# Two heads per transpose and four tiles per product group in the chunked scan of a two-block model

## The reference, cut to what matters

```python
def wkv_scan(s0, r, decay, k, v, kk, b, reverse, emit):
    def step(s, inp):
        r_t, w_t, k_t, v_t, kk_t, b_t = inp
        sa = jnp.einsum('bhij,bhj->bhi', s, kk_t)
        s = s * w_t[:, :, None, :] - sa[..., None] * b_t[:, :, None, :] + v_t[..., None] * k_t[:, :, None, :]
        y = jnp.einsum('bhij,bhj->bhi', s, r_t) if emit else None
        return s, y
```

## Time and profile before

| What | us |
|---|---|
| median of 3 executions | 4247.13 (4242.57 to 4247.59) |
| the profiled execution, its own time | 4238.4 |
| its span, first to last instruction | 4236.3 |
| scan stage, first sums to last output copy | about 1808 to 2387 of the span |
| PE busy over the whole span | 3841.8 (91%) |
| DVE, ACT, POOL busy | 1773.6, 1452.8, 699.4 |

### The profile page before, as it was taken

One profiled execution on the slowest core, in us unless ns is written; L12 is line 12 of the kernel. 1 busy time (PEld: TensorE's weight loads), 2 busy tenths in 40 slices (PEclk: granted clock), 3 DMA queues, 4 the chain that ended last, 5 costly groups with the idle time before them and its releaser, 6 DMA issues. The chain is left out here.

```text
span 4236.3 us, 83925 instructions
## 1 busy us (share of the span) xinstructions
PE 3841.8 (91%) x35190; PEld 3279.1 (77%) x35190; DVE 1773.6 (42%) x3239; ACT 1452.8 (34%) x3109; POOL 699.4 (17%) x573
## 2 busy tenths in 40 slices
PE   8999989899899987589999779798969889999998
PEld 2789988777789986388999658678956678888886
DVE  3323344555543123845545468652134451111234
ACT  2111167555531112633333340152126552121133
POOL 0000065110100095133433351110000000000001
PEclk9999999999999998799999789899979999999999
DMA  8223363110522375632222341232252221111121
GB/s 356 72 85 113 105 133 75 31 43 8 207 87 83 114 232 191 267 83 61 65 66 73 104 145 40 92 144 84 88 175 56 100 104 46 50 46 48 37 94 72
DMA packets 293220, 431.47 MB, mean 102 GB/s; under 512 B 76725, under 2 KB 216597, under 8 KB 288577
## 3 DMA queue, kind: packets, MB, share of 16 engines
q1 hardware_dynamic: 292586, 421.42, 31.3%
q10 hardware_dynamic: 288, 5.07, 0.3%
HBM read 307.38 MB, written 124.03 MB: 102 GB/s over the span
## 5 line engine op out<-in xcount | busy, mean ns | idle before, releaser
L416 PE MATMUL g_acc<-g_wh,l_x_high 128*128 128x320 f32 (+5 forms) x1824 | 590.2, 324 | 12.3 <-DVE g_o L464 6.6
L416 PE MATMUL g_acc<-g_wh,l_x_low 128*128 128x320 f32 (+5 forms) x1824 | 588.5, 323 | 0.0
L416 PE MATMUL g_acc<-g_wl,l_x_high 128*128 128x320 f32 (+5 forms) x1824 | 588.5, 323 | 0.0
L416 PEld LDWEIGHTS g_acc<-g_wh,l_x_high 128*128 128x128 f32 x1824 | 345.2, 189 | 19.3 <-DVE g_o L464 6.9
L416 PEld LDWEIGHTS g_acc<-g_wl,l_x_high 128*128 128x128 f32 x1824 | 345.7, 190 | 2.8
L416 PEld LDWEIGHTS g_acc<-g_wh,l_x_low 128*128 128x128 f32 x1824 | 345.0, 189 | 2.3
L440 ACT COPY g_o<-g_acc 128x320 f32<-128x320 f32 (+6 forms) x120 | 54.5, 454 | 771.6 <-PE g_acc L416 757.4
L464 DVE COPY g_o<-g_acc 128x320 f32<-128x320 f32 (+6 forms) x120 | 62.6, 524 | 576.1 <-PE g_acc L416 547.6
L3247 PE MATMUL ffi_acc<-l4a_x_high,ffi_wh 128*128 128x512 f32 x704 | 274.3, 390 | 0.2 <-DVE ffi_wl L54 0.2
L3247 PE MATMUL ffi_acc<-l4a_x_high,ffi_wl 128*128 128x512 f32 x704 | 274.1, 389 | 0.0
L3247 PE MATMUL ffi_acc<-l4a_x_low,ffi_wh 128*128 128x512 f32 x704 | 274.1, 389 | 0.0
(11 more groups left out here) (516 smaller groups left out, 9071.4 us busy)
## 6 DMA issues: line engine op xcount, KB each, us to landing
scan_F<-s_FE SPq DMA_DIRECT2D x160, 192.0 KB, 3.8
s_FE<-feat_f SPq DMA_DIRECT2D x10, 2304.0 KB, 7.8
l4a_first_w<-in_w_ffn_in SPq DMA_DIRECT2D x44, 512.0 KB, 3.8
g_cu<-s_U SPq DMA_DIRECT2D x24, 768.0 KB, 5.2
pj_o<-s_O SPq DMA_DIRECT2D x26, 512.0 KB, 4.4
front_w<-in_attn_ada_w SPq DMA_DIRECT2D x8, 1536.0 KB, 10.9
front_w<-in_rec_ada_w SPq DMA_DIRECT2D x8, 1536.0 KB, 12.2
g_wr<-in_w_ffn_out SPq DMA_DIRECT2D x44, 256.0 KB, 2.7
```

The source lines that it names most:

```text
L416: mm = pe.matmul(acc[r][:, 0:it["n"]], left, right, start=(k == 0 and q == 0), stop=(k == kt - 1 and q == 2))
```

## The change

PE's part of the scan is rewritten; the other engines' code stays as it is, except that DVE clears `side` in place of `one`.

- The transposes take two heads at once, a 128x128 block in one instruction: 4 in place of 16 per tile. Of two neighbouring pairs the channels now lie on the halves by the pair's parity, and the half that the tokens had chooses the place along the free dimension. `own` lists the heads whose tokens and channels lie on the same half, `cross` the others.
- The products that go from channels to tokens or back use the tiles of the array that fit: own heads those on the diagonal, cross heads the two others. `grams` is split in two halves, a and b, each of which has own heads for one bank beside cross heads for the other bank.
- `sums` uses all 128 rows and columns: one product with `tri` and two of two columns with `side`, in place of two and eight.
- mix_w, mix_s and mix_y are cut into an own part and a cross part, with a semaphore that PE sets and waits for itself between them (`w_half`, `s_half`, `y_half`, `gram_half`), and the order of the loop changes.

```diff
+own = [(b, 2 * j + b) for j in range(NP2 // 2) for b in range(2)]
+cross = [(b, 2 * j + 1 - b) for j in range(NP2 // 2) for b in range(2)]
+
+def tok(b, h):
+    return HALF[b], slice(h * C, (h + 1) * C), h
+
+def chan(b, h):
+    g = h - h % 2 + b
+    return HALF[h % 2], slice(256 + g * C, 256 + (g + 1) * C), g
...
-    for hb in HALF:
-        pe.matmul(b[0][hb, 0:256], tri[hb, 2 * d, hb], flat(f[hb, 3, :, :]), start=True, stop=True)
-    for h in range(NP2):
-        mm = pairs(b[0], 256 + h, 1, f[:, 3, h, :], one[:, :])
+    pe.matmul(b[0][:, 0:256], tri[:, 2 * d, :], flat(f[:, 3, :, :]), start=True, stop=True)
+    for j in range(NP2 // 2):
+        mm = pe.matmul(b[0][:, 256 + 2 * j:258 + 2 * j], flat(f[:, 3, 2 * j:2 * j + 2, :]), side[:, :], start=True, stop=True)
...
-            for h in range(NP2):
-                for hb in HALF:
-                    mm = pe.matmul(b[to][hb, x * 256 + h * C:x * 256 + (h + 1) * C], left[hb, x, h, :], ident[hb, hb], start=True, stop=True)
+            for j in range(NP2 // 2):
+                mm = pe.transpose(b[to][:, x * 256 + j * P:x * 256 + (j + 1) * P], flat(left[:, x, 2 * j:2 * j + 2, :]), ident[:, :])
...
-def grams(n, d):
-    s, b = e[d], bank[d]
+def gram(n, d, x, b, h):
+    ch, _, g = chan(b, h)
+    return pe.matmul(bank[d][2 * x][HALF[b], h * P:(h + 1) * P], KB[d][ch, x, g, :], AR[d][n % 2][ch, g, :, :].rearrange("p x t -> p (x t)"), start=True, stop=True)
+
+def grams_a(n, d):
+    s = e[d]
     pe.wait_ge(s["a_out"], n + 1)
     pe.wait_ge(s["kb_out"], n + 1)
     pe.wait_ge(s["exps"], 4 * n + 4)
-    for x, to in ((1, 2), (0, 0)):
-        for h in range(NP2):
-            mm = pairs(b[to], h * P, P, KB[d][:, x, h, :], AR[d][n % 2][:, h, :, :].rearrange("p x t -> p (x t)"))
-        mm.then_inc(s["grams"], 1)
+    for i in (0, 2):
+        for x, some in ((1, own), (0, cross)):
+            for b, h in some[i:i + 2]:
+                mm = gram(n, d, x, b, h)
+    mm.then_inc(s["gram_half"], 1)
+
+def grams_b(n, d):
+    s = e[d]
+    pe.wait_ge(s["gram_half"], n + 1)
+    for i in (0, 2):
+        for x, some in ((1, cross), (0, own)):
+            for b, h in some[i:i + 2]:
+                mm = gram(n, d, x, b, h)
+            if i == 2:
+                mm.then_inc(s["grams"], 1)
...
+        for b, h in cross:
+            t, to, _ = tok(b, h)
+            pe.matmul(b3[t, to], gk[t, h, 0, :], f[t, 1, h, :], start=(h < 2), stop=False)
+        for b, h in own:
+            t, to, _ = tok(b, h)
+            pe.matmul(b3[t, to], ar[t, chan(b, h)[2], 0, :], st0[t, chan(b, h)[2], :], start=False, stop=False)
+        for b, h in own:
+            t, to, _ = tok(b, h)
+            mm = pe.matmul(b3[t, to], gk[t, h, 0, :], f[t, 1, h, :], start=False, stop=False)
+        mm.then_inc(s["w_half"], 1)
+    for d in range(2):
+        s, b3, ar, st0 = e[d], bank[d][3], AR[d][n % 2], S[d][n % 2]
+        pe.wait_ge(s["w_half"], n + 1)
+        for b, h in cross:
+            t, to, _ = tok(b, h)
+            ch, _, g = chan(b, h)
+            mm = pe.matmul(b3[t, to], ar[ch, g, 0, :], st0[ch, g, :], start=False, stop=(h >= 2))
         mm.then_inc(s["w_mm"], 1)
...
-def mix_s(n):
-    for d in range(2):
-        s, b, f = e[d], bank[d], F[d][n % 3]
-        pe.wait_ge(s["u_out"], n + 1)
-        for h in range(NP2):
-            pairs(b[3], 256 + h * C, C, qk[d][n % 2][:, 0, h, :], f[:, 1, h, :], True, False)
-            mm = pairs(b[3], 256 + h * C, C, qk[d][n % 2][:, 1, h, :], Un[d][:, h, :], False, True)
-        mm.then_inc(s["s_mm"], 1)
-
-def mix_y(n, d, h):
-    s, b = e[d], bank[d]
+def mix_s(n, d, some):
+    s, b3, f = e[d], bank[d][3], F[d][n % 3]
+    pe.wait_ge(s["u_out"] if some is own else s["s_half"], n + 1)
+    for i in (0, 2):
+        for b, h in some[i:i + 2]:
+            ch, to, _ = chan(b, h)
+            pe.matmul(b3[ch, to], qk[d][n % 2][HALF[b], 0, h, :], f[HALF[b], 1, h, :], start=True, stop=False)
+        for b, h in some[i:i + 2]:
+            ch, to, _ = chan(b, h)
+            mm = pe.matmul(b3[ch, to], qk[d][n % 2][HALF[b], 1, h, :], Un[d][HALF[b], h, :], start=False, stop=True)
+    mm.then_inc(s["s_half"] if some is own else s["s_mm"], 1)
+
+def mix_y(n, d):
+    s, b3, ar, st0 = e[d], bank[d][3], AR[d][n % 2], S[d][n % 2]
+    pe.wait_ge(s["s_out"], n + 1)
+    pe.wait_ge(s["gr"], n + 1)
+    for b, h in cross:
+        t, to, _ = tok(b, h)
+        ch, _, g = chan(b, h)
+        mm = pe.matmul(b3[t, to], ar[ch, g, 1, :], st0[ch, g, :], start=(h < 2), stop=False)
+    mm.then_inc(s["y_half"], 1)
+
+def mix_y_rest(n, d, h):
+    s, b3, ar, gk, gr, f, st0 = e[d], bank[d][3], AR[d][n % 2], GK[d][n % 2], GR[d][n % 2], F[d][n % 3], S[d][n % 2]
     if h == 0:
-        pe.wait_ge(s["s_out"], n + 1)
-        pe.wait_ge(s["gr"], n + 1)
-    pairs(b[3], h * C, C, AR[d][n % 2][:, h, 1, :], S[d][n % 2][:, h, :], True, False)
-    pairs(b[3], h * C, C, GK[d][n % 2][:, h, 1, :], F[d][n % 3][:, 1, h, :], False, False)
-    mm = pairs(b[3], h * C, C, GR[d][n % 2][:, h, :], Un[d][:, h, :], False, True)
+        pe.wait_ge(s["y_half"], n - CCH + 1)
+    t, to, _ = tok(h % 2, h)
+    pe.matmul(b3[t, to], ar[t, chan(h % 2, h)[2], 1, :], st0[t, chan(h % 2, h)[2], :], start=False, stop=False)
+    pairs(b3, h * C, C, gk[:, h, 1, :], f[:, 1, h, :], False, False)
+    mm = pairs(b3, h * C, C, gr[:, h, :], Un[d][:, h, :], False, h == NP2 - 1)
     if h == NP2 - 1:
         mm.then_inc(s["ys_mm"], 1)
-pieces = {0: ((0, 0), (0, 1), (0, 2), (0, 3)), 2: ((1, 0),), 4: ((1, 1),), 5: ((1, 2),), 6: ((1, 3),)}
+pieces = {0: ((0, 0), (0, 1)), 1: ((0, 2), (0, 3)), 2: ((1, 0),), 4: ((1, 1),), 5: ((1, 2),), 6: ((1, 3),)}
...
-        grams(n, 0)
+        grams_a(n, 0)
     if n:
-        mix_s(n - 1)
+        mix_s(n - 1, 0, own)
+        mix_s(n - 1, 1, own)
     if n < NCH:
-        grams(n, 1)
+        grams_b(n, 0)
+    if n:
+        mix_s(n - 1, 0, cross)
+        mix_s(n - 1, 1, cross)
+    if n < NCH:
+        grams_a(n, 1)
+    if n and emits(n - 1):
+        mix_y(n - 1, 0)
+    if n < NCH:
+        grams_b(n, 1)
+    if n and emits(n - 1):
+        mix_y(n - 1, 1)
     for k in range(8):
...
             step(n, k)
         for d, h in pieces.get(k, ()):
             if n and emits(n - 1):
-                mix_y(n - 1, d, h)
+                mix_y_rest(n - 1, d, h)
```

More of the change, by code:

```diff
@@ L1439, in rwkv_scan_stage @@
         masks = st.sb("masks", [P, 10, C])
-        one = st.sb("one", [P, 1])
+        side = st.sb("side", [P, 2])
         unit = st.sb("unit", [P, C])
@@ L1469, in rwkv_scan_stage @@
             "loaded0_", "loaded1_", "loaded2_", "sums", "exps", "shifted", "scaled", "turned", "a_out", "kb_out", "grams", "ga", "g_out", "gr", "gk", "parts",
-            "step_a", "step_b", "power", "r_out", "ss_out", "tt_out", "w_mm", "w_out", "u_mm", "u_out", "s_mm", "ys_mm", "y_out", "s_sum", "s_out",
+            "step_a", "step_b", "power", "r_out", "ss_out", "tt_out", "gram_half", "w_half", "s_half", "y_half", "w_mm", "w_out", "u_mm", "u_out", "s_mm", "ys_mm", "y_out", "s_sum", "s_out",
             "stored0_", "stored1_")} for d in range(2)]
@@ L1610, in mix_w @@
                     for d in range(2):
-                        s, b = e[d], bank[d]
+                        s, b3, ar, gk, f, st0 = e[d], bank[d][3], AR[d][n % 2], GK[d][n % 2], F[d][n % 3], S[d][n % 2]
                         pe.wait_ge(s["gk"], n + 1)
@@ L1616, in mix_w @@
                                 pe.wait_ge(s["y_out"], n - CCH)
-                        for h in range(NP2):
-                            pairs(b[3], h * C, C, AR[d][n % 2][:, h, 0, :], S[d][n % 2][:, h, :], True, False)
-                            mm = pairs(b[3], h * C, C, GK[d][n % 2][:, h, 0, :], F[d][n % 3][:, 1, h, :], False, True)
+                        for b, h in cross:
[15 more added lines that the diff above has]
+                            mm = pe.matmul(b3[t, to], ar[ch, g, 0, :], st0[ch, g, :], start=False, stop=(h >= 2))
                         mm.then_inc(s["w_mm"], 1)
@@ L1640, in mix_y @@
-                def mix_y(n, d, h):
-                    s, b = e[d], bank[d]
-                    if h == 0:
-                        pe.wait_ge(s["s_out"], n + 1)
-                        pe.wait_ge(s["gr"], n + 1)
-                    pairs(b[3], h * C, C, AR[d][n % 2][:, h, 1, :], S[d][n % 2][:, h, :], True, False)
-                    pairs(b[3], h * C, C, GK[d][n % 2][:, h, 1, :], F[d][n % 3][:, 1, h, :], False, False)
-                    mm = pairs(b[3], h * C, C, GR[d][n % 2][:, h, :], Un[d][:, h, :], False, True)
+                def mix_s(n, d, some):
[9 more added lines that the diff above has]
+                    mm.then_inc(s["s_half"] if some is own else s["s_mm"], 1)
@@ L1771, in _ @@
                 pool.wait_ge(const_in, 32)
-                pool.wait_ge(cleared, 5)
+                pool.wait_ge(cleared, 7)
                 for d in range(2):
@@ L1805, in _ @@
             def _(dve):
```

(5 more changed lines are left out.)

2 lines of the change are left out of this document (1 added, 1 removed).

## The result

The changed kernel takes 4262.15 us (median of 6, 4254.53 to 4265.21), the kernel before, beside it, 4244.07 (4239.76 to 4247.59). The ratio is 1.0042, 95% interval 1.003 to 1.0054: slower, by some 18 us. The forecast was 4242, no change. The profiled execution after spans 4261.3 us.

A forecast was written before the change was run, and what follows sets the result against it. Two things bound an iteration: PE's work and the chain from the second gram through ACT, POOL and DVE. 16 iterations at +0.29 and 5 at -1.9 sum to -5 us: 4233 profiled, median 8.7 above, so 4242; range 4212 to 4275.

The forecast's parts named there:

- The wait that is added: PE at mix_y(n-1, 0), now ahead of grams_b(n, 1), waits for DVE's `s_out`: 2.3 us idle; step 2 +0.49 net.
- the signs to look for: scan_S waits about 2.3 us in 15 iterations, transposes at 0.109, grams under 0.03, iterations 29.0 and 25.8, PE busy 3 us less.
- another case: Rival B, gram records staying at 0.0547, put the time at 4262; the range left out only its tail with D.
- The walk: One iteration timed from the end of mix_w: GA(0) 5.38, mix_y 8.91, GA(1) 9.83, step 1 12.86, step 2 13.9.
- the forecast's case: Rival A: the wait at mix_y eats PE's gain; 4242 us, its own range 4228 to 4257; chance 0.53.
- Transposes, grams: PE per iteration: transposes 1.87 to 1.19 per direction, gain 1.36; grams 3.50 to 1.87 at 0.0292 per record, gain 1.63.
- Rival B: The four tiles do not run together, gram records stay at 0.0547: +20 us, 4262; chance 0.25.
- Sums: PE's sums go from 0.87 to 0.93 us with a switch in and out: 0.06 more each, 0.12 in all.
- C: PE's saving goes through, 3.07 us in 20 iterations, -61: 4186; needs state ahead of transposing R; chance 0.12.
- D: Tiling switches or PE's waits on itself cost their upper ends, +0.3 and +0.3 an iteration: +12, 4255 and above; chance 0.10.
- The chances (0.32, 0.37, 0.31): Chances that the changed kernel is faster (0.32), the same (0.37) or slower (0.31).

The follow-up runs named there:

- the filled kernel: Changed kernel with unread identity products in PE's idle time: 30 ahead of mix_y(n-1, 0), 24 ahead of step 1 of d = 1, 16 after grams_b without output; 4240.68 us.
- the best version: Also "the fastest version": changed kernel with DVE's state before start(n, 0), mix_y(n-1, 0) behind grams_b(n, 1), and identity products, 14 ahead of step 1; 4210.68 us (4215.95 without fill).
- the kernel before with 0.89 us put in: Kernel before, PE waiting for the state of d = 0 ahead of grams(n, 1), mix_y pieces of d = 0 moved behind step 1 of d = 1; 4273.55 us.
- the changed kernel with the first stretch filled: Changed kernel with 30 identity products ahead of mix_y(n-1, 0), 16 after grams_b(n, 1) without output, none ahead of step 1 of d = 1; 4249.98 us.
- two other versions of the kernel before: Kernel before with only DVE's order changed, state before start(n, 0), 4243.03 us; and with PE waiting for the state of d = 1 ahead of grams(n, 1), 4287.28 us.
- the kernel with reordered products: Changed kernel with gram products reordered, all own heads into one bank, then all cross heads into the other; 4259.24 us.
- the state first: Changed kernel with DVE making the state of chunk n-1 before it transposes R of chunk n (start(n, 0) behind state(n-1)); 4216.31 us.

## Why the prediction was wrong

**What failed** is the step "The wait that is added". It found two idle stretches of PE, of 2.3 and almost 2 us, and priced them as time alone. What they do to the granted clock stands in no term of the sum, in none of the rivals and in none of the signs to look for, although have the clock as a column. It is 19.3 of the 21.4 us that the stretch gained; the filled kernel shows it, and the kernel before with an idle stretch put in shows that the change's own products aren't needed for it. Why the clock falls in one iteration and not in the next stays open. The Trainium skill ("TensorE: Matmul & The Clock Gate", Part 1) names idle time as what lowers this clock, and its example has longer waits than these; the prediction cited the page for another rule and didn't weigh this one. Its range (4212 to 4275) held the result only because another case reached as far.

**The walk** was right, up to step 2. From the end of mix_w: GA of d = 0 at 5.03 (forecast 5.38), mix_y at 8.61 (8.91), GA of d = 1 at 9.55 (9.83), step 1 of d = 1 at 12.58 (12.86), step 2 at 13.64 in the filled kernel (13.9). All are 0.3 early from the first copy on. The wait for the state is 2.26 (2.3). Iterations at full clock: 29.24 with output (29.0) and 25.85 without (25.8). And the filled kernel, which is the forecast's case without the clock, takes the time of before.

**Transposes, grams.** 0.49 from one block of four to the next and 0.54 from the second to mix_u: 1.03 for a direction (1.19). Gram records run at 0.055 with two tiles and at half with four. Rival B said 4262 and the result is 4262, by coincidence: its mechanism is false. That also settles the rule of the Trainium skill that the prediction set against the trace ("TensorE: Matmul & The Clock Gate", Part 3, that a weight load overlaps a running matmul only where the row groups differ): own and cross heads share a row group, and their records run side by side. Measurement decides; the rule doesn't hold here.

**Sums** were mis-sized: +0.06 forecast. Without output, from the first record of one sums to that of the next it is 4.54 in the filled kernel and 4.32 before, and this holds one block of sums and its two switches: +0.22. With output it is 4.89 and 4.68. In the timeline of PE of the filled kernel (the earlier trace rows before):

```profile
2076.85 0.28 PE L1535 MATMUL scan_bank<-scan_Un,scan_GR 64*64 64x64 f32 x3
2077.06 0.70 PE L1556 MATMUL scan_bank<-scan_F,scan_tri 128*128 128x256 f32 x2
2077.60 0.50 PE L1558 MATMUL scan_bank<-scan_side,scan_F 128*128 128x2 f32 x4
2078.03 0.68 PE L1535 MATMUL scan_bank<-scan_M,scan_SS 64*64 64x64 f32 x16
```

Three records ahead of the sums take 0.09, so without a switch the triangular product would start at 2076.94; it starts at 2077.06, and the next follows 0.54 later: 0.66 in all, where the forecast had 0.43 and 0.175 for the switch. The four records of two columns with the switch back take 0.43, where it had 0.24 and 0.09. Two such blocks are 0.32 over the forecast, and from step 2 to the end an iteration takes 15.60 (29.24 - 13.64) where the forecast had 15.1. So they are most of this difference, and step 2 coming 0.26 early hides half of it.

**Rivals C and D.** C had named its condition, the state ahead of the transposing of R, and this is what the best version does; of its 61 us 25 to 33 came, since POOL bounds next. D's +0.3 for the switches came close in size: around the transposes they were cheaper than forecast, and the sums with theirs cost 0.32 more. The chances (0.32, 0.37, 0.31) left room for slower, but for the wrong reasons.

## What to carry to other kernels

An idle stretch of PE has two prices: its own length, and the slower clock of the work after it. The second does not come every time: here the clock fell after the same stretches in some iterations and not in others. When a change shortens PE's work but leaves a chain on other engines, look at the lengths of the gaps that it makes, and at the clock column of the windows of before and after, before pricing any product. Then either remove the wait by reordering the queue that it stands in (here one line on DVE, 46 us), or, where it can't go, put products whose results nobody reads into the gap, shorter than the gap. In the fastest version this brought 5 us with 16 products after the grams without output and 14 ahead of step 1, and nothing with 28 ahead of step 1 (4218.36, for 4215.95 with none).

## What was not expected of the hardware

- The clock: after idle stretches of about 1.8 to 2.3 us between full work, it was at half for 6.8 us in the iteration shown, in some iterations and not in others of the same kernel with the same stretches. Shorter ones can do it as well: without output 1.30 and 1.49 us, close together, left 0.94 in all four iterations of the fastest version without fill (27.15 for 25.85). What stays open is why stretches of up to 1.73 us never did this with output in the kernel before (0 of 28) and one of 1.76 did in the changed one in 4 of 14. Without output, a stretch of 1.72 us left the clock at 1.00 in all four iterations of the kernel before with 0.89 us put in, and one of 1.74 us at 0.94 in all four of the changed kernel with the first stretch filled; but in two other versions of the kernel before it fell once. The length is not all, and whether the kind of work or the position in time adds to it, these runs don't tell.
- PE doesn't start records in the order of the program where they use different tiles: gram records of the next block started while those of mix_s, which the program has ahead of them, were still to come (2068.93 and 2068.97 in the kernel with reordered products):

```profile
2068.91 0.23 PE L1674 MATMUL scan_bank<-scan_F,scan_qk 64*64 64x64 f32 x2
2068.93 0.33 PE L1577 MATMUL scan_bank<-scan_AR,scan_KB 64*64 64x128 f32 x2
2068.97 0.23 PE L1674 MATMUL scan_bank<-scan_F,scan_qk 64*64 64x64 f32 x2
```

- With the state first, DVE's scaling of the state of d = 0 overlaps POOL's masking and takes 0.83 us where it takes 0.42 in the kernel before, and POOL's `mid` takes 0.91 for 0.73. That the overlap is the reason is likely, but nothing else was tried. DVE, then POOL, in that kernel:

```profile
2062.01 0.83 DVE L1929 TENSOR_TENSOR scan_S<-scan_S,scan_eT 128x256 f32<-128x256 f32 x1
```

```profile
2063.39 0.91 POOL L1834 TENSOR_TENSOR scan_mid<-scan_GA,scan_masks 128x256 f32<-128x256 f32 x1
```

- A 128x128 f32 transpose costs 0.12 us less than the same block as a f32 product with the identity (29.22 against 31.14 us per iteration, which has 16).
